# Expert matmuls with the roles of the operands exchanged: token slots stationary, expert weights moving

## The reference, cut to what matters

```python
def swiglu(h, w13, w2):
    gate, up = jnp.split(h @ w13, 2, axis=-1)
    return (jax.nn.silu(gate) * up) @ w2

def moe_swiglu(h, router, w13, w2):
    t = h.reshape(B * S, D)                       # 256 x 1024
    logits = (t @ router).astype(jnp.float32)
    top_val, top_idx = lax.top_k(logits, TOP_K)   # 2 of 8
    gate = jax.nn.softmax(top_val, axis=-1)
    combine = jnp.einsum('tk,tke->te', gate, jax.nn.one_hot(top_idx, N_EXPERTS))
    out = jnp.zeros_like(t)
    for e in range(N_EXPERTS):
        out = out + combine[:, e:e + 1] * swiglu(t, w13[e], w2[e])
```

## Time and profile before

| | us |
|---|---|
| median of 3 runs (lowest, highest) | 2100.55 (2094.56, 2102.69) |
| the profiled execution's own time | 2093.34 |
| its span, first to last instruction | 2091.4 |
| PE busy in the span | 1883.4 |
| DVE, ACT, POOL busy | 523.7, 260.7, 198.3 |
| from the first matmul of expert 0 to the last of expert 7 | 1050.2 |

### The profile page before, as it was taken

One profiled execution on the slowest core, in us unless ns is written; L12 is line 12 of the kernel. 1 busy time (PEld: TensorE's weight loads), 2 busy tenths in 40 slices (PEclk: granted clock), 3 DMA queues, 4 the chain that ended last, 5 costly groups with the idle time before them and its releaser, 6 DMA issues.

```text
span 2091.4 us, 58343 instructions
## 1 busy us (share of the span) xinstructions
PE 1883.4 (90%) x27004; PEld 1536.6 (73%) x27004; DVE 523.7 (25%) x1305; ACT 260.7 (12%) x558; POOL 198.3 (9%) x318
## 2 busy tenths in 40 slices
PE   8999998999989999989888887988879888889987
PEld 4445454877735587776788887988879888889987
DVE  2132132000063657753401112011120110111110
ACT  2122122000002254432000000000000000000000
POOL 1111110100011336420000000000000000000000
PEclk9999999999999999999899999999999999999999
DMA  9442441644531011023598987989888889899992
GB/s 364 142 149 81 143 138 64 198 157 140 161 121 36 11 19 31 16 83 145 218 383 332 347 325 291 392 324 338 320 328 338 333 327 338 330 338 398 392 374 99
DMA packets 137717, 473.96 MB, mean 227 GB/s; under 512 B 30105, under 2 KB 59057, under 8 KB 94465
## 3 DMA queue, kind: packets, MB, share of 16 engines
q1 hardware_dynamic: 134592, 460.05, 59.6%
q0 software_dynamic: 2080, 7.37, 1.1%
q10 hardware_dynamic: 800, 2.76, 0.4%
HBM read 460.04 MB, written 10.10 MB: 225 GB/s over the span
## 4 chain that ended last, share of the span: by engine, by line
PE 82%; issue 7%; DVE 6%; ACT 2%; DMA 2%; SPq 0%; POOL 0%; DVEq 0%; POOLq 0%
PE ps L685 28%; PE ps L1267 14%; PE ps L676 12%; PE ps L799 12%; PE ps L737 7%; PE ps L750 3%; PE ps L853 1%; PE ps L766 1%; DMA arena<-yd,arena 1%; PE ps L1197 1%; DVE arena L1871 1%; PE ps L1204 1%; PE ps L784 1%; DMA arena<-wqkv 0%; PE ps L961 0%
## 5 line engine op out<-in xcount | busy, mean ns | idle before, releaser
L685 PE MATMUL ps<-arena 128*64 128x96 f32 (+1 forms) x15104 | 655.3, 245 | 91.2 <-issue 88.4
L685 PEld LDWEIGHTS ps<-arena 128*64 128x64 f32 x15104 | 631.0, 136 | 114.3 <-issue 110.2
L676 PE MATMUL ps<-arena 128*128 128x128 f32 (+11 forms) x2114 | 332.3, 331 | 32.6 <-DVE arena L1858 9.2
L1267 PE MATMUL ps<-arena 128*64 128x96 f32 x7168 | 317.6, 245 | 39.2 <-issue 37.6
L1267 PEld LDWEIGHTS ps<-arena 128*64 128x64 f32 x7168 | 304.3, 135 | 47.5 <-issue 47.5
L676 PEld LDWEIGHTS ps<-arena 128*128 128x128 f32 (+4 forms) x2114 | 247.5, 186 | 109.0 <-issue 55.4
L799 PE MATMUL ps<-arena 128*128 128x512 f32 x576 | 253.0, 595 | 1.7 <-DMA arena<-wqkv 1.7
L2133 DVE TENSOR_TENSOR arena<-arena,ps 128x192 f32<-128x192 f32 x112 | 39.5, 355 | 754.3 <-ACT arena L1563 754.3
L799 PEld LDWEIGHTS ps<-arena 128*128 128x128 f32 x576 | 108.0, 191 | 128.3 <-issue 125.6
L737 PE MATMUL ps<-arena 128*128 128x256 f32 x704 | 153.6, 381 | 0.0
L737 PEld LDWEIGHTS ps<-arena 128*128 128x128 f32 x704 | 134.4, 191 | 20.1 <-issue 1.9
(11 more groups left out here) (246 smaller groups left out, 999.4 us busy)
## 6 DMA issues: line engine op xcount, KB each, us to landing
arena<-mw SPq DMA_DIRECT2D x336, 1024.0 KB, 8.0
arena<-wqkv SPq DMA_DIRECT2D x36, 1024.0 KB, 7.4
arena<-fw SPq DMA_DIRECT2D x32, 1024.0 KB, 6.7
arena<-wrkv SPq DMA_DIRECT2D x12, 1024.0 KB, 7.3
arena<-awo SPq DMA_DIRECT2D x4, 1024.0 KB, 6.2
arena<-bwo SPq DMA_DIRECT2D x4, 1024.0 KB, 10.0
xg<-arena POOLq DMA_DIRECT2D x8, 384.0 KB, 9.4
arena<-xg SPq DMA_DIRECT2D x7, 384.0 KB, 9.8
```

The source lines that it names most:

```text
L676: last = mm(o, a, b, start=(n == 0), stop=(n == len(pairs) - 1))
L685: last = mm(o[c], a[:, c], b, start=(n == 0), stop=(n == len(pairs) - 1))
L1267: last = mm(ps[c, 5 + o // 4, o % 4 * width:(o % 4 + 1) * width], w[:, k, o * P + c.start:o * P + c.stop], hidT[:, g % 2, k, 0:width], sta ...
```

## The change

Token slots become the stationary operand and the weights move. Slots 0 to 63 take half of the array's columns at a time (COLS), slots 64 to 95 a quarter (QUADS). The halves and quarters work on different weight columns. The hidden layer and the result then have slots on the partitions: the hidden layer must be turned (turned(), 16 DVE transposes for two up units), the result no longer.

```diff
+COLS = (slice(0, RH), slice(RH, P))
+QUADS = tuple(slice(32 * a, 32 * a + 32) for a in range(4))
@@ tensor engine, expert(): an up unit
-                        for f in range(4):
-                            last = by_halves(ps[:, g % 4, f * width:(f + 1) * width],
-                                             [(w[:, k, f * P:(f + 1) * P], picked[:, b, k, 0:width]) for k in range(KB)])
+                        for k in range(KB):
+                            for a, r in enumerate(COLS):
+                                mm(ps[r, g % 4, 0:256], picked[:, b, k, 0:64], w[:, k, a * 256:(a + 1) * 256], start=(k == 0), stop=(k == KB - 1))
+                        for k in range(KB):
+                            for a, r in enumerate(QUADS):
+                                last = mm(ps[r, g % 4, 256:384], picked[:, b, k, 64:CAP], w[:, k, a * P:(a + 1) * P], start=(k == 0), stop=(k == KB - 1))
                         last.then_inc(up_ps, 1)
@@ a down unit
-                        pe.wait_ge(hide_sb, n * GE + (2 * g + 2))
-                        if g == 0:
-                            pe.wait_ge(yT_sb, n * 2 + 2)
-                        for o in range(KB):
-                            for k in range(4):
-                                for c in COLS:
-                                    last = mm(ps[c, 5 + o // 4, o % 4 * width:(o % 4 + 1) * width], w[:, k, o * P + c.start:o * P + c.stop],
-                                              hidT[:, g % 2, k, 0:width], ...
+                        pe.wait_ge(hidT_sb, n * (GE // 2) + (g + 1))
+                        if first:
+                            pe.wait_ge(y_sb, n * 2 + 2)
+                        for k in range(4):
+                            for a, r in enumerate(COLS):
+                                mm(ps[r, 5, :], hidT[:, g % 2, k, 0:64], w[:, k, a * 512:(a + 1) * 512], ...
+                        for k in range(4):
+                            for a, r in enumerate(QUADS):
+                                last = mm(ps[r, 6, 0:256], hidT[:, g % 2, k, 64:CAP], w[:, k, a * 256:(a + 1) * 256], ...
-            def result_rows(n, width):   # the turning of the last result on PE goes
@@ scalar engine, expert()
-                    act.activation(sg_e[:, g % 2, 0:2 * width], ps[:, g % 4, 0:2 * width], ACT.Silu).then_inc(sge_sb, 1)
+                    act.activation(sg_e[RH:P, g % 2, :], ps[0:RH, g % 4, 0:3 * P], ACT.Silu).then_inc(sge_sb, 1)
-                act.wait_ge(y_sb, n * 2 + 2)
-                for half in range(2):
-                    act.activation(yT[:, 4 * half:4 * half + 4, 0:width], ps[:, 5 + half, 0:4 * width]..., ACT.Copy).then_inc(yT_sb, 1)
+                act.wait_ge(yd_out, stored)
+                for a, r in enumerate(COLS):
+                    last = act.activation(yb[0:RH, a * 512:(a + 1) * 512], ps[r, 5, :], ACT.Copy)
+                last.then_inc(y_sb, 1)
@@ vector engine
+            def turned(pair):
+                last = None
+                for i in range(2):
+                    q = RH + 32 * i
+                    low = hid_e[q:q + 32, pair % 2, :, 0:256].rearrange("p a (f j c) -> p a f j c", j=4, c=32)
+                    high = hid_e[q:q + 32, pair % 2, :, 256:384].rearrange("p a (j c) -> p a j c", j=4)
+                    for j in range(4):
+                        o = hidT[32 * j:32 * j + 32, pair % 2].rearrange("p (a f) n -> p a f n", f=2)
+                        dve.transpose(o[:, :, :, 32 * i:32 * i + 32], low[:, :, :, j, :])
+                        last = dve.transpose(o[:, :, i, 64:CAP], high[:, :, j, :])
+                return last
@@ vector engine, expert()
-                    if g % 2 == 0 and pair >= 2:
-                        dve.wait_ge(down_ps, n * (GE // 2) + (pair - 1))
-                    dve.tensor_tensor(hidT[:, pair % 2, ...], sg_e[:, g % 2, 0:2 * width]..., ps[:, g % 4, 2 * width:4 * width]..., ALU.mult).then_inc(hide_sb, 1)
+                    dve.tensor_tensor(hid_e[RH:P, pair % 2, g % 2, :], sg_e[RH:P, g % 2, :], ps[RH:P, g % 4, 0:3 * P], ALU.mult).then_inc(hide_sb, 1)
+                    if g % 2:
+                        dve.wait_ge(hide_sb, n * GE + (g + 1))
+                        if pair >= 2:
+                            dve.wait_ge(down_ps, n * (GE // 2) + (pair - 1))
+                        turned(pair).then_inc(hidT_sb, 1)
                     if g == 1 and at_second:
                         at_second()
-                    if g in (9, 11) and next_b is not None:
-                        next_picked(n, next_b, (g - 9) // 2)
+                    if g in (8, 10) and next_b is not None:
+                        next_picked(n, next_b, (g - 8) // 2)
+                dve.wait_ge(down_ps, n * (GE // 2) + GE // 2)
+                dve.wait_ge(yd_out, stored)
+                for a, r in enumerate(QUADS):
+                    last = dve.tensor_copy(yb[RH:CAP, a * 256:(a + 1) * 256], ps[r, 6, 0:256])
+                last.then_inc(y_sb, 1)
-            def result_rows(n):          # the 24 transposes of the result go, and last_rows, first_rows
```

More of the change, by code:

```diff
@@ L227, in build @@
         picked = m.take(2, KB, P)
-        yT = m.take(KB, P)
-        sg_e = m.take(2, 256)
+        hid_e = m.take(2, 2, 3 * P)
+        sg_e = m.take(2, 3 * P)
         hidT = m.take(2, 4, P)
@@ L1260, in expert @@
                         w = unit(u).rearrange("p (k n) -> p k n", n=D)
-                        pe.wait_ge(hide_sb, n * GE + (2 * g + 2))
-                        if g == 0:
-                            pe.wait_ge(yT_sb, n * 2 + 2)
-                        for o in range(KB):
-                            for k in range(4):
-                                for c in COLS:
-                                    last = mm(ps[c, 5 + o // 4, o % 4 * width:(o % 4 + 1) * width], w[:, k, o * P + c.start:o * P + c.stop],
-                                              hidT[:, g % 2, k, 0:width], start=(g == 0 and k == 0 and o % 4 == 0),
-                                              stop=(g == GE // 2 - 1 and k == 3), skip_group_check=True)
-                        last.then_inc(down_ps, 1)
-            def result_rows(n, width):
-                for half in range(2):
[L1275 to L1278, removed]
+                        first, end = g == 0, g == GE // 2 - 1
+                        pe.wait_ge(hidT_sb, n * (GE // 2) + (g + 1))
[3 more added lines that the diff above has]
+                            for a, r in enumerate(COLS):
+                                mm(ps[r, 5, :], hidT[:, g % 2, k, 0:64], w[:, k, a * 512:(a + 1) * 512],
+                                   start=(first and k == 0), stop=(end and k == 3), skip_group_check=True)
+                        for k in range(4):
+                            for a, r in enumerate(QUADS):
+                                last = mm(ps[r, 6, 0:256], hidT[:, g % 2, k, 64:CAP], w[:, k, a * 256:(a + 1) * 256],
+                                          start=(first and k == 0), stop=(end and k == 3), skip_group_check=True)
+                        last.then_inc(down_ps, 1)
             pe.wait_ge(pick_ok, 2)
@@ L1305, in _ @@
                     pick_transposes(n + 1, 0, j + 3)
[L1306 to L1310, removed]
+                    gather_half(0, 0, CAP)
+                    gather_half(0, 1, CAP, j + 2)
+                    expert(n, n + 1, 0, over_plan, landed)
+                    scatter(n, 0, j + 2, CAP)
         @block.scalar
@@ L1555, in pickT_out, with expert @@
                 act.activation(pickT[:, b].rearrange("p t n -> p (t n)"), ps[:, 4, 0:S], ACT.Copy).then_inc(pickT_sb, 1)
-            def expert(n, width, before_last=None):
+            def expert(n, stored, before_last=None):
                 for g in range(GE):
@@ L1598, in _ @@
                     pickT_out(j + 2, 0)
-                    expert(j + EXPERTS, P)
-                    first_rows(j + EXPERTS, j + 1, P)
+                    expert(j + EXPERTS, EXPERTS * 16)
         @block.vector
@@ L2099, in next_picked @@
                 dve.tensor_tensor(picked[:, b, ks, 0:CAP], picked[:, b, ks, 0:CAP], gain_of(half, CAP), ALU.mult).then_inc(picked_sb, 1)
-            def result_rows(n):
[L2103 to L2116, removed]
             def add_back(c, weight):
```

48 lines of the change are left out of this document (15 added, 33 removed).

## The result

| | before | after |
|---|---|---|
| median of the runs, us (lowest, highest) | 2101.62 (2094.56, 2108.25) | 1986.92 (1984.76, 1988.34) |
| profiled execution's own time, span | 2093.34, 2091.4 | 1985.81, 1983.9 |
| expert stage, first to last matmul | 1050.2 | 943.7 |
| PE idle in the stage | 127.7 | 17.1 |

The changed kernel takes 0.9454 of the time of before (95% interval 0.9421 to 0.9487), 114.7 us less. In the profiled executions the span is 107.5 us shorter, 106.5 of it in the expert stage; the rest of the difference of the medians is how the two profiled executions lie in their runs.

What follows compares the result with a forecast made beforehand. PE was taken to wait for its program code, one gap per packet. Stage: 934 (units) + 5 + 2.4 + 5 + 17 = 964 us; 2093.3 - 87 = 2006, median 7.2 higher, 2014; own range 1980 to 2050, whole range to 2090.

Steps and rivals of the forecast that it cites:

- code: PE in the expert stage: packets last 8.9 us on average after the change, so it hardly waits; 5 us left.
- the turning: DVE transposes of the hidden layer: 4.5 us a pair, hidden except before down 6, costing 2.4 us in all.
- the loop turns: PE at two loop turns: idle time and half clock stay as before, 17 us.
- the stall at expert 7: PE before down 1 of expert 7, while DVE waits for yd's way out and back: 5 us kept.
- the weights' rate: Rival, weight loads: memory gives only 338 GB/s for long, 168 units take 1042 us, nothing won, 2100 us; chance 0.08.
- a fixed price per packet: Rival, PE's code: each packet costs 0.9 + 0.2 us whatever the pace, 116 us in all, 2125 us; chance 0.08.
- The period of 6.2 us: Code queue in the kernel before: one packet per 6.2 us, taken as the pace the fetch has shown.
- Quarters: Matmuls in four column groups: 27.9 ns a record, so 64 records of an up unit take 1.79 us.
- The end of 37.0 ns: Rival, quarters' records: 37.0 ns each, the smallest interval in any row, +65 us, 2079 us; dearer-quarters chance 0.15.
- the rival of two at a time: Quarters run only two side by side, up-unit records 54.6 ns apart, +285 us, 2299 us; chance 0.10.
- Changes of shape: PE going from halves to quarters and back once a unit: 0.34 us; ends nothing and twice that, +57 us.
- The lower end: Times under 1980 us: weight loads would bind, at 396 GB/s 5.3 us a unit, 5.4 with small traffic.

Runs made afterwards that it cites:

- (4): The kernel before with 104 moving columns in place of 96 in the experts' matmuls, 8 of them zeros, same instruction count: 2052.24 us, ratio 0.9875.
- (1): The changed kernel with moving operands cut into pieces of 128 columns, 256 instructions a unit again: 2027.06 us, ratio 0.972 to the kernel before.
- (3): The kernel before with about half of the weight bytes moved for experts 2 to 7, same program: 1989.20 us, ratio 0.9595.
- (2): The changed kernel with only the down units cut into pieces of 128 columns, 4480 instructions an expert: 1993.37 us, ratio 0.9593 to the kernel before.
- 5: The kernel before with PE's loop turns written out: 2042.47 us, ratio 0.9761.
- (7): The changed kernel with the order of halves and quarters reversed in every second unit: 1969.63 us.
- (6): The changed kernel with halves and quarters alternating at each k-block of the up units: 2212.06 us, ratio 1.0693 to the kernel before.
- experiment 8: The changed kernel with PE's three loop turns over experts 0 to 5 written out: 1967.58 us, against 1985.48.
- 10: The changed kernel with alternating order, add_rows moved to expert 7's eighth product and PE's loop turns written out: 1947.48 us, ratio 0.9419 to the kernel before.

## Why the prediction was right

The time of 1986.92 us lies in the range and in the forecast's own range (1980 to 2050), 27 us under the 2014 forecast. The mechanism held; the sum took units, code and the turning 14, 5 and 2.4 us too high, and only the loop turns and the stall at expert 7 2.5 us too low. Step by step:

- **What bounded the kernel.** That PE waited for its own code, one gap a packet, is shown: PE resumes 2.4 us after each packet's start (4), the gaps come back with the instructions (1), go with half of the weight traffic (3), and 8% more work in the same code makes the kernel faster (4). That the count of instructions alone sets the gain is not: with the count of before some 50 us of gain stay (1), and the pace of a packet has its share (4). Nor are the exchanged roles tested by themselves: no run has them with 5.28 us of work a packet. The rivals that needed another bound, the weights' rate or a fixed price per packet, are out: the changed kernel takes weights at 397 GB/s for 190 us, and 35 more packets an execution cost 6 to 8 us (2).
- **The period of 6.2 us** was taken for what a fetch can do. It isn't a constant: 5.3 us with half of the weights beside it, 5.7 in the wide kernel with nearly all, and 6.4 where the code is not ahead. The conclusion (8.9 us a packet is slow enough) held because it stood above all of them; in up units, with 256 / 192 x 5.49 = 7.3 us a packet, the margin is 0.9 us. For packets of 5.3 to 5.7 us, as in experiments 1, 4 and 5, the same argument gave wrong numbers.
- **Quarters.** Four column groups do run side by side. 64 records take 1.88 us with one change of shape of 0.15 in it, so 27.0 ns each; the next 64 in a row add 3.63 - 1.88 = 1.75 us, 27.3 ns each (7). Both are under the 27.9 taken, next to pure streaming. The end of 37.0 ns and the rival of two at a time are out.
- **Changes of shape.** 0.34 us a unit was predicted from two PE transposes; 0.30 is measured (6). With the quarters' smaller price a unit is 5.49 and 5.45 us in place of 5.58 and 5.52. Over 168 units that is 14 us, the largest part of the error.
- **Code.** 5 us were left for it; PE's waits show none outside the loop turns (four by "issue", 12.9 us, two at each turn).
- **DVE.** The turning was taken as 4.5 us a pair; the two transposes take 0.44 us together, 3.6 a pair. So down 6 never waits, and 2.4 us of the forecast were not there. The stall at expert 7 was 4.2 us idle and 2.4 more in the part behind it, which took 6.02 us in place of 3.58 at a granted clock of 0.63 (1889 to 1896 us); 5 stood for it, and removing it gave 7.8.
- **Loop turns.** 17 us predicted, 17.9 by experiment 8.
- **The lower end.** "Lower than 1980 the loads bind" was wrong, though this result doesn't touch it: versions of this kernel run at 1969.63 and 1947.48 us (7, 10), with 402 and 407 GB/s.
- **The sum.** 8 x (14 x 5.49 + 7 x 5.45) = 920 us, 18 of loop turns and 6.6 at expert 7 are 945, measured 943.7, predicted 964. The other 6 us of the 27 are the step from the profiled execution to the median: 7.2 before, 1.1 after.

**What stays open.** Why the fetch of code falls behind and stays behind in one stretch, and keeps up in another at the same pace and the same DMA load (before_unroll, split_all), was not settled. It comes down to one packet started early or not, and the loop turns start one early; what does it elsewhere isn't known. The trace shows when a packet moves, not when it was asked for.

## What to carry to other kernels

Look for idle time of PE that nothing explains and count the instructions between two gaps: if it is constant and a code packet goes with each, a remedy is fewer instructions for the same columns, that is longer moving operands. Less traffic beside the code ended the gaps too; deeper buffers for the weights were not tried, and PE wasn't waiting for weights. Where the array is used in column groups of two widths, put all matmuls of one width together and let neighbouring groups of work meet in the same width. Write out the loop turns of the engine that bounds: it gained 17.9 us here (8), and did no harm in the kernel before, whose code was late already (5).

## What the runs showed of the hardware

- Program code reaches PE in packets of 16 KB (256 instructions) over the core's 16 DMA engines, beside the weights. A packet moved in some 1 us. Beside 340 to 400 GB/s of weights packets came mostly 5.3 to 7 us apart, and where PE waited for each, it resumed 2.4 us after the packet's start and the next one started 4.0 us later. A program of 5376 instructions per 111 us of work lost 126 us of its 1050 us stage to idle time by "issue", 14 of them at the loop turns.
- PE's jump back at a loop turn cost 4.0 + 1.8 us of idle time at the first turn and 5.5 + 1.6 at the second, and a stretch at 1.2 GHz behind it, some 9 us a turn in all (8). The granted clock is 0.94 from 1250 to 1280 us and 1.00 on either side, and the first 24 records behind the gap take 4.50 us, where 32 take 3.60 otherwise. The Trainium skill, TensorE: Matmul & The Clock Gate, What's actually happening ("The two states you'll see"), names that clock as the lower of two, and these records agree.
- Four column groups of 32 with float32 operands run at once, 27.0 to 27.3 ns a record of 128 columns where pure streaming is 26.7, beside weights arriving at 397 GB/s.
- A change between column groups of 64 and of 32 costs 0.13 to 0.15 us. That is what the Trainium skill, TensorEngine Tiling (Array Packing), Key Properties, leads one to expect of a change of tiling mode; it gives no price.
- One core, running alone, was given 397 GB/s from memory for 190 us, and 402 and 407 for 400 and 300 us in the fastest version. The Trainium skill, DMA: Bandwidth & Descriptors, Specifications, states some 358, as half of what two cores share; for one core alone the measurement decides.
